# Expert rows gathered per token against expert tables streamed once, in the PEER layers of a two-block network on one core

## The reference

```python
def _peer(h, w_q, k1, k2, u_tab, v_tab):           # h: 256 tokens x 1024; u_tab, v_tab: 16384 x 1024
    q = (h @ w_q).reshape(b, l, PEER_HEADS, 2, PEER_HALF)        # 8 heads, two halves of 128
    s1 = einsum('blhc,hnc->blhn', q[..., 0, :], k1)              # 128 keys each
    s2 = einsum('blhc,hnc->blhn', q[..., 1, :], k2)
    v1, i1 = top_k(s1, 16);  v2, i2 = top_k(s2, 16)
    cand_s = v1[..., :, None] + v2[..., None, :]                 # 256 pairs
    cand_i = i1[..., :, None] * 128 + i2[..., None, :]
    top_s, pos = top_k(cand_s, 16)
    idx = take_along_axis(cand_i, pos);  g = softmax(top_s)
    # per token t, over its 8 x 16 = 128 picked experts e:
    a = gelu(u_tab[idx] . h_t);   y_t = sum_e g_e * a_e * v_tab[idx_e]
```

## Time and profile before

| | |
|---|---|
| Time, median of 3 runs (range) | 2646.77 us (2644.35 to 2647.7) |
| The profiled execution's own time | 2644.71 us |
| Its span in the trace | 2642.9 us |
| PE, DVE, ACT, POOL busy | 88%, 58%, 28%, 22% of the span |
| Mean granted TensorE clock | 0.981 of 2.4 GHz |
| DMA, read from HBM | 774.8 MB, 294 GB/s over the span |

### The profile page before, as it was taken

One profiled execution on the slowest core, in us unless ns is written; L12 is line 12 of the kernel. 1 busy time (PEld: TensorE's weight loads), 2 busy tenths in 40 slices (PEclk: granted clock), 3 DMA queues, 4 the chain that ended last, 5 costly groups with the idle time before them and its releaser, 6 DMA issues.

```text
span 2642.9 us, 24167 instructions
## 1 busy us (share of the span) xinstructions
PE 2321.8 (88%) x8140; PEld 1485.7 (56%) x8140; DVE 1527.7 (58%) x3681; ACT 742.8 (28%) x2120; POOL 586.3 (22%) x526
## 2 busy tenths in 40 slices
PE   8999999999989998998997777777889987778776
PEld 6678888876878886566443333322674433233222
DVE  3743642255446412446777678776447677777774
ACT  2232100122220003324333333432324333333332
POOL 0000000000000000003443544534014443534531
PEclk9999999999999999999999999999999999999999
DMA  7315587442438754217999999999649999999996
GB/s 294 129 36 219 190 311 267 176 152 80 162 117 311 299 192 153 110 64 297 420 420 419 418 412 421 406 420 421 248 182 421 420 420 421 416 414 415 411 421 259
DMA packets 92317, 777.43 MB, mean 294 GB/s; under 512 B 10273, under 2 KB 11425, under 8 KB 11937
## 3 DMA queue, kind: packets, MB, share of 16 engines
q0 software_dynamic: 73728, 536.90, 49.2%
q1 hardware_dynamic: 18464, 238.99, 23.8%
HBM read 774.80 MB, written 1.05 MB: 294 GB/s over the span
## 4 chain that ended last, share of the span: by engine, by line
DMA 27%; PE 18%; POOL 7%; DVE 5%; issue 3%; ACT 2%; ACTq 0%
DMA weight_ring<-tables,arena 16%; DMA arena<-tables,arena 11%; PE misc L1355 6%; POOL arena L1511 4%; POOL weight_ring L1511 3%; PE tile L295 3%; PE tile L1281 3%; PE tile L308 2%; DVE weight_ring L1485 1%; DVE arena L1485 1%; PE tile L1631 1%; PE tile L1630 1%; PE misc L1654 1%; PE tile L318 1%; ACT arena L1437 0%
## 5 line engine op out<-in xcount | busy, mean ns | idle before, releaser
L1355 PE MATMUL misc<-arena 128*128 128x512 f32 x1216 | 582.0, 615 | 140.4 <-ACT arena L1437 140.4
L1511 POOL DMA_INDIRECT arena<-tables,arena x304 | 327.1, 1076 | 1037.1 <-DVE arena L1133 887.3
L1355 PE MATMUL misc<-weight_ring,arena 128*128 128x512 f32 x832 | 395.0, 613 | 110.7 <-ACT arena L1437 110.4
L1485 DVE CUSTOM_DVE_ANT_0 arena<-arena,memT 128x1024 f32<-128x1024 f32 x304 | 371.2, 1224 | 186.8 <-DMA arena<-tables,arena 183.9
L1355 PEld LDWEIGHTS misc<-arena 128*128 128x128 f32 x1216 | 224.8, 193 | 430.4 <-ACT arena L1437 226.2
L295 PE MATMUL tile<-xT,weight_ring 128*128 128x256 f32 x1792 | 388.6, 379 | 0.0
L295 PEld LDWEIGHTS tile<-xT,weight_ring 128*128 128x128 f32 x1792 | 340.3, 190 | 47.9 <-issue 1.8
L1511 POOL DMA_INDIRECT weight_ring<-tables,arena x208 | 256.3, 1232 | 426.3 <-DVE arena L1133 363.3
L1485 DVE CUSTOM_DVE_ANT_0 weight_ring<-weight_ring,memT 128x1024 f32<-128x1024 f32 x208 | 254.2, 1224 | 150.5 <-DMA weight_ring<-tables,arena 149.7
L1355 PEld LDWEIGHTS misc<-weight_ring,arena 128*128 128x128 f32 x832 | 151.1, 192 | 328.1 <-ACT arena L1437 185.8
L1423 ACT ACTIVATE arena<-arena 128x2 f32<-128x2 f32 x256 | 52.2, 204 | 812.3 <-DVE arena L1485 812.2
(11 more groups left out here) (257 smaller groups left out, 2279.8 us busy)
## 6 DMA issues: line engine op xcount, KB each, us to landing
weight_ring<-panels SPq DMA_DIRECT2D x110, 2048.0 KB, 7.9
arena<-tables,arena POOLq DMA_INDIRECT x304, 15.0
weight_ring<-tables,arena POOLq DMA_INDIRECT x208, 18.8
arena<-c_rows SPq DMA_DIRECT2D x2, 1024.0 KB, 21.1
cst<-consts SPq DMA_DIRECT2D x1, 1224.0 KB, 26.8
xT<-acts SPq DMA_DIRECT2D x1, 1024.0 KB, 5.0
memT<-acts SPq DMA_DIRECT2D x1, 1024.0 KB, 11.5
arena<-acts SPq DMA_DIRECT2D x1, 1024.0 KB, 6.6
```

What stands on the lines that cost most here:

```text
L1355: ins = nc.tensor.matmul(M[2 * a + b][:, :], diag[:, s % NDIAG, :], slot(rows, s)[:, D + b * 512:D + (b + 1) * 512], start=first_row, stop ...
L1485: nc.vector.tensor_tensor_reduce(out=u, in0=u, in1=ht[:, n // PH, :], scale=1.0, scalar=0.0, op0=ALU.mult, op1=ALU.add, accum_out=dot[:, c ...
L1511: pool.indirect_dma_start(slot(rows, s), None, tables, bass.IndirectOffsetOnAxis(idx[:, n % 2, k:k + 1], 0)).then_inc(landing(rows, s), 16)
```

## The change

The table of experts is no longer gathered. It is laid out on the host as "halves" of 1 MB (128 partitions x 8 KB), each with the u or the v rows of two "cells"; a cell holds the 128 experts that share i2, one on each value of i1. There are 128 cells and so 128 halves a layer. SP streams all of them (`load_halves`) through a ring of four, and TensorE computes gelu(U h) for all 16384 experts and 256 tokens (`up`) and the product with V (`down`). Between them the result is multiplied by a dense gate matrix, [128 values of i1] x [128 cells] for each token, that is zero but for the picked experts. It is made for each token as a product of two one-hot matrices over the token's 128 picks: hot_a[pick, i1] = gate, hot_b[pick, i2] = 1 (`batch`: four tokens in one PSUM bank). POOL, DVE and ACT make the one-hot matrices.

```diff
+HALF = PANEL // 2
+HALVES = 4
+NX = NCELL // 2
+XP = NX // 2
+PARKED = 4
+LAST_HALVES = 4
+TURN_BESIDE = 13
+FIRST_BATCH = 14
+BATCH = 4
+BATCHES = P // BATCH
+DEEP = 3
+DVE_HOT = (2, 3)
+        def peer_pe(e, rd, l, nth):
...
+            def up_step(p, w, i, k):
+
+                bank = e.bank("u", u0 + p) if i == k == 0 else T_[e.tiles.at("u", u0 + p)[0]]
+                c = (i * KD + k) * P
+                ins = nc.tensor.matmul(bank[:, i * T:(i + 1) * T], w[:, c:c + P], hp[:, k, :],
+                                       start=(k == 0), stop=(k == KD - 1))
...
+            def turn(a):
+                pe.wait_ge(sem("gate_ready"), TT * l + a + 1)
+                bank = e.bank("turn", TT * l + a)
+                for i in range(3):
+                    ins = nc.tensor.transpose(bank[:, i * P:(i + 1) * P], sel[:, a, i, :], ident)
...
+            def batch(b):
+
+                pe.wait_ge(sem("hot_dve"), b0 + b + 1)
+                pe.wait_ge(sem("hot_pool"), b0 + b + 1)
+                pe.wait_ge(sem("hot_act"), b0 + b + 1)
+                if b >= NBANK:
+                    pe.wait_ge(sem("batch_read"), b0 + b - NBANK + 1)
+                for i in range(BATCH):
+                    s = b % DEEP * BATCH + i
+                    ins = nc.tensor.matmul(batch_bank(b)[:, i * P:(i + 1) * P], hot_a[:, s, :], hot_b[:, s, :],
+                                           start=True, stop=True)
+                ins.then_inc(sem("batch_made"), 1)
+
+            def down_step(w, p, i, b, first, last):
+                a, d = divmod(b, 2)
+                return nc.tensor.matmul(M[b][:, :], cell(cells(p)[i])[:, a, :], w[:, i * D + d * 512:i * D + (d + 1) * 512],
+                                        start=first, stop=last)
...
+            e.several_tiles(e.panel("pq", 4 * l), "pq", range(q0, q0 + 4), KD, hp, T,
+                            lambda k: pe.wait_ge(sem("hp_made"), KD * l + k + 1))
...
+            for p in range(XP):
+                up(p)
+                if p == TURN_BESIDE:
+                    turn(0)
+                if FIRST_BATCH <= p < FIRST_BATCH + BATCHES // 2:
+                    for b in range(2):
+                        batch(2 * (p - FIRST_BATCH) + b)
+            turn(1)
+            for b in range(BATCHES):
+                batch(BATCHES + b)
+                for m in range(2 * b, 2 * b + 2):
+                    p, step = XP + m // (2 * KD), m % (2 * KD)
+                    if step == 0:
+                        w = e.half()
+                    up_step(p, w, step // KD, step % KD)
+            pe.wait_ge(sem("cells_x_made"), BATCHES * (l + 1))
+            pe.wait_ge(sem("batch_read"), TT * BATCHES * (l + 1))
+            for p in range(XP):
+                down(p)
+                if p < XP - PARKED:
+                    up(XP + PARKED + p)
+            for p in range(XP, 2 * XP - LAST_HALVES):
+                down(p)
...
+            def one_hot(b):
+                if b >= DEEP:
+                    act.wait_ge(sem("batch_made"), b0 + b - DEEP + 1)
+                act.wait_ge(sem("apart_made"), b0 + b + 1)
+                nc.scalar.activation(hot_b[:, b % DEEP * BATCH + BATCH - 1, :], apart[:, b % 2, :], ACT.Relu, scale=-1.0,
+                                     bias=1.0).then_inc(sem("hot_act"), 1)
+                if (b + 1) % BATCHES:
+                    distance(b + 1)
...
+            def cells_second(b):
+                dve.wait_ge(sem("batch_made"), b0 + BATCHES + b + 1)
+                at = X[:, 1, :, b * BATCH:(b + 1) * BATCH]
+                nc.vector.tensor_tensor(at, by_cell(batch_bank(BATCHES + b))[:, NX:2 * NX, :], at, ALU.mult
+                                        ).then_inc(sem("cells_x_made"), 1)
...
+            for n in range(PH):
+                choice(n)
+            below_top(0)
+            choice(8)
+            normalised(0)
+            choice(9)
+            for n in range(10, HEADS):
+                choice(n, 4)
+            assert made == BATCHES
+            below_top(1)
+            normalised(1)
+            for q in range(4):
+                cells_first(q)
+            for i in range(DEEP):
+                one_hot()
+            for b in range(BATCHES):
+                cells_second(b)
+                if made < TT * BATCHES:
+                    one_hot()
+            for p in range(XP):
+                weighted(p)
...
+        def peer_pool(pool, rd, l):
+            b0 = TT * BATCHES * l
+            for b in range(TT * BATCHES):
...
+                for i in range(DVE_HOT[b // BATCHES], BATCH):
+                    nc.gpsimd.tensor_scalar(hot_a[:, s + i, :], iota, selT_flat[:, t + i:t + i + 1],
+                                            selT_flat[:, 2 * T + t + i:2 * T + t + i + 1], ALU.is_equal, ALU.mult)
+                for i in range(BATCH - 1):
+                    ins = nc.gpsimd.tensor_scalar(hot_b[:, s + i, :], iota, selT_flat[:, T + t + i:T + t + i + 1], None,
+                                                  ALU.is_equal)
+                ins.then_inc(sem("hot_pool"), 1)
```

More of the change, by code:

```diff
@@ L162 @@
[L162 to L192, removed]
@@ L519, in clear_semaphores @@
         def clear_semaphores():
-            names = [name for name in sems if not name.startswith("row_landed")]
+            names = list(sems)
             def clear(eng, part):
@@ L1059, in build_program @@
-        far = ring[:, :].rearrange("p (s n) -> p s n", s=RING - HOME)
-        def slot(rows, s):
-            kind, i = rows.place[s]
-            return (near if kind == "near" else far)[:, i, :]
-        def landing(rows, s):
-            kind, i = rows.place[s]
-            return sem(f"row_landed{i if kind == 'near' else HOME + i}")
-        scores = cut(P_MEM, "s12", "p (n b k) -> p n b k", n=TT * PH, b=2)
-        wk = cut(P_MEM, "wk", "p (b n) -> p b n", b=2)
-        v16 = cut(P_MEM, "v16", "p (b k) -> p b k", b=2)
@@ new lines, in peer_pe @@
+            for p in range(XP, 2 * XP - LAST_HALVES):
+                down(p)
+            last = [(p, e.half()) for p in range(2 * XP - LAST_HALVES, 2 * XP)]
+            pe.wait_ge(sem("weighted"), XP * (l + 1))
+            for n, b in enumerate(CLOSING):
+                for p, w in last:
+                    for i in range(2):
+                        ins = down_step(w, p, i, b, False, p == 2 * XP - 1 and i == 1)
+                ins.then_inc(sem("bank_summed"), 1)
+                if n == 2:
+                    pe.wait_ge(sem("closed_dve"), TT * l + 1)
+                    pe.wait_ge(sem("closed_act"), TT * l + 1)
+                    for f in range(4):
+                        for a in range(TT):
+                            turned_back(f, a)
@@ new lines, in peer_act @@
+            gate_exp(1)
+            turn(1)
+            distance(BATCHES)
+            for b in range(BATCHES, BATCHES + DEEP):
+                one_hot(b)
+            for b in range(BATCHES):
+                copy_second(b)
+                if b + DEEP < BATCHES:
+                    one_hot(BATCHES + b + DEEP)
+            for p in range(XP):
+                gelu_y(p)
+            for d in range(2):
+                act.wait_ge(sem("bank_summed"), 4 * l + 2 * d + 2)
+                nc.scalar.activation(closed[:, 1, d * 512:(d + 1) * 512], M[2 + d][:, :], ACT.Copy
+                                     ).then_inc(sem("closed_act"), 1)
@@ new lines, in load_halves @@
+                def load_halves(l, beside=None):
+                    for n in range(len(HALF_ORDER)):
+                        name, p = HALF_ORDER[n - HALVES]
+                        if n < HALVES:
+                            rd.full("pq", 16 * l + (7 if n < 2 else 11))
+                        elif name == "u":
+                            rd.full("u", 2 * XP * l + p)
+                        else:
+                            sp.wait_ge(sem("down_used"), (2 * XP - LAST_HALVES) * l + p + 1)
+                        if beside and n >= HALVES:
+                            beside(name, p)
+                        s = n % HALVES
+                        sp.dma_start(ring[:, s * HALF:(s + 1) * HALF],
+                                     halves[bass.ds(len(HALF_ORDER) * l + n, 1)].rearrange("a p c -> (a p) c")
+                                     ).then_inc(sem(f"half_landed{s}"), 16)
```

881 lines of the change are left out of this document (420 added, 461 removed).

## The result

The changed kernel takes 3403.97 us (median of 4 runs, 3403.07 to 3405.67). The kernel before, run beside it, takes 2647.23 us (4 runs, 2644.35 to 2648.16). The ratio is 1.286, 95% interval 1.284 to 1.288: slower by 757 us, where the prediction had a gain of 263. The forecast, its range and its sign are all wrong.

A forecast was written before the change was run, and what follows sets the result against it. The prediction held the PEER layers bound by gather transfers, 640 us a layer. Its steps summed to 558 us against 689.5 (layer 0) and 564 against 695.4 (layer 1), a gain of 263: 2384 us, range 2330 to 2475.

The forecast's parts named there:

- Price of a matmul: TensorE price in the dense work: 0.215 us for 256 columns, 0.429 for 512, so about 3.44 us a half.
- TensorE's spare room: In the kernel before, little TensorE work was needed beside the gather: 128 query, 32 score and 512 row matmuls a layer.
- (a): Start of a layer, queries and scores in one piece, all on the path: 32 us.
- (b): `up` of 32 halves, 110.1 us, with the first 32 batches beside it, 15.4 us; TensorE alone done at 158 us.
- (c): DVE's own chain of selections, decodes, one-hots and softmax: 169 us, setting the end of this part; POOL starts at 172.
- (d): The second 32 batches, led by POOL at 1.56 us a batch: 50 us, ending at 224 us.
- Rival 1: POOL and DVE exclude each other, or one-hots cost more: 38 us a layer more, 2460 us in all; chance 0.24.
- (e): The remaining 28 `up` and 64 `down` halves, 92 x 3.44 = 316.5 us, to 540 us.
- (f): Close of a layer: 16 us plus 2 us of `kept` activations in layer 0, 24 us in layer 1.
- The stream at nothing: Streaming of halves costs no time: 2.7 us a half, covered by TensorE's 3.44 us a half.
- Rival 3: The ring of four 1 MB halves starves TensorE: 50 us a layer more, 2485 us in all; chance 0.07.
- Rival 4: Slower than before: POOL's `tensor_scalar` near 0.955 us, 148 us a layer more, 2680 us; decided from 0.90 us each; chance 0.04.

## Why the prediction was wrong

**The failed step is "Price of a matmul".** It read "465 in 100 us, 0.215 us each" and "0.429 each" as prices of a product. They are steps from one record to the next, and an fp32 product has two records. Products cost 0.43 and 0.86 us, a half 6.88. The section weighed the rule of the Trainium skill (page "FP8 and Floating Point Precision", TensorE Precision Notes: true fp32 takes four passes) and dismissed it with "the trace disagrees, as 0.215 us for 256 columns at 2.4 GHz is two cycles a column". The runs agree with the Trainium skill here: 0.43 us is four cycles a column, and the bf16 product beside it takes about one (1.1). The estimate given by it, some 440 us more a layer, was close to what came: 509 and 511 us.

The trace of before held the answer. The earlier trace rows has x1440 records of PE in a layer; the prediction counted 128 + 32 + 512 = 672 products, twice that is 1344, and transposes and sums are the rest. The profile page of before has 1216 + 832 = 2048 records for the 1024 row products of both layers:

```profile
L1355 PE MATMUL misc<-arena 128*128 128x512 f32 x1216 | 582.0, 615 | 140.4 <-ACT arena L1437 140.4
...
L1355 PE MATMUL misc<-weight_ring,arena 128*128 128x512 f32 x832 | 395.0, 613 | 110.7 <-ACT arena L1437 110.4
```

And "a panel of 2 MB goes with 32 matmuls" took 465 records for products of 15 panels: in the panel list every second one there is a `mod` panel, which TensorE skips (L268). Seven `fi` panels of 32 products are 224 products, 448 records.

By its steps, in layer 0:
- Bound by transfer before: right (half of the products leave the time the same). TensorE's spare room: wrong, 1.72 of about 2.5 us a step were taken.
- (a) 65 for 32: the price, twice.
- (b), (c) 255 for 140. Twice the price makes (b) 32 x 6.88 + 32 x 8 x 0.12 = 251. TensorE, not DVE's chain, sets its end; DVE had been idle for 24.8 us when the last gates came. So the 169 us of (c) were not put to the test. Their 6.65 us a selection also leave out the 0.2 us of the cast between its two parts (1961.78 to 1961.99 in the earlier trace rows).
- (d) 90 for 52. Here POOL's price failed by itself: 0.79 and 0.60 us, where twice a memset, 0.39, was taken. 0.79 + 3 x 0.60 leads with 2.53 us a batch, and the wait beside `cells_first` adds 10 us. Rival 1 named this exclusion by the Trainium skill's page "SBUF — State Buffer" (SBUF: two separate sides), and the row of 5.52 us shows POOL shut out so, over more than one DVE instruction, though it is worth a few us of 509. DVE's one-hot took 0.33 to 0.39, not 0.22.
- (e) 642 for 316.5: 92 x 6.88 = 633, the largest part.
- (f) 16 for 18: right (the last row matmul ends at 1866.8 by the earlier trace rows, not 1866.7).
- The stream at nothing: right. TensorE waited 10.2 us for halves in all; that says little by itself, as a half took 6.88 us and not 3.44, but with half of the products, at 3.44, it waited 10.0. Rival 3 fell.

The differences 33 + 115 + 38 + 325 - 2 make 509 us. Rival 4 had the sign but not the cause: POOL's instructions stayed under 0.90 us on average (0.87 and 0.64) and led only in the second batches. No rival said that a product could cost twice; the one rule that did was given no chance, although it decided the sign. By the corrected price alone the change takes a layer from a 2.5-us gather step times 256, 640 us, to 128 halves x 6.88 = 881 us of TensorE, and can't win in fp32. With the price put right POOL's one-hots come next: the run with half of the products, where POOL works through the batches without a gap, shows that the forecast would have missed its range by them as well. It takes 2618 us; without the 33 us a layer that its queries cost too much that is 2552, an estimate, against the 2475 at which the range ends.

## What to carry to other kernels

Before a duration or a step from a trace is used as a price, divide the group's count by the number of products that the code issues there; for the fp32 products here the quotient is two, and a step of 0.215 us stands for half a product. Replacing gathered rows by dense work on all rows pays where the dense product is cheap: in this kernel 0.91 of the time with bf16 high parts (0.88 with the one-hots moved to DVE as well), at less precision, and 1.29 with fp32. When a stated rule and one's reading of a row disagree by a factor of two, give the rule a rival's chance, or find a second row (a count, a byte ratio) that decides it.

## What the runs showed that was not expected

- **The clock falls with the work.** In the same 596 us of gathering, with the same time, the mean granted clock was 0.99 with all row products, 0.79 with half of them and 0.57 with bf16 ones. These are means over two levels: in the run with half, 1430 to 1435 us is at 1.00 (2.4 GHz) and 1405 to 1410 at 0.50 (1.2 GHz). The fp32 512-column record went from 613 to 800 ns and more. So taking work away frees less busy time than its price, and a busy share is to be read beside its clock; with the row products twice the same window is at 1.00. This agrees with the Trainium skill, page "TensorE: Matmul & The Clock Gate" (Part 1: The HAM clock gate): the clock follows how busy the engine has been.
- **A bf16 view of fp32 data** with a step of two elements takes 0.117 us for 256 columns, 1.1 cycles a column at a granted clock of 1.00, and 8 records of 512 columns take 1.98 us.
- **POOL's `tensor_scalar`** of 128 columns costs 0.60 us with one operation and 0.79 with two, against 0.33 on DVE, and a memset of the same size 0.205: a memset is no measure for it.
